# Opening of a two-sublayer decoder kernel on one core: four weight blocks in four equal strips in place of three blocks in five

## What is computed

```python
cond = silu(c)
mod = cond @ ada_w + ada_b                      # 2048 -> 9 * 2048
sh1, sc1, gt1, sh2, sc2, gt2, sh3, sc3, gt3 = split(mod, 9)
x = sandwich(x, swiglu(., ffn1_w_in, ffn1_w_out), sh1, sc1, gt1, 0.5)
x = sandwich(x, token_mixer(...),                 sh2, sc2, gt2, 1.0)
x = sandwich(x, swiglu(., ffn2_w_in, ffn2_w_out), sh3, sc3, gt3, 0.5)
# sandwich: x + res_w * gate * rms_norm(fn(rms_norm(x) * (1 + scale) + shift))
# swiglu(h): gate, up = split(h @ w_in, 2); (silu(gate) * up) @ w_out, hidden width 5504
```

## Time and profile before

| what | value |
|---|---|
| median of three timed runs | 1901.06 us (1900.74 to 1901.34) |
| the profiled execution's own time | 1902.87 us |
| its span, first to last instruction | 1901.1 us |
| busy: TensorE (PE), VectorE (DVE), ScalarE (ACT), GpSimd (POOL) | 98%, 77%, 45%, 4% |
| mean granted TensorE clock | 0.992 of full |
| read from memory over the span | 483.31 MB, 255 GB/s |

### The profile page before, as it was taken

The page is one execution under the profiler, slowest core; times in us unless marked ns, Lnnn a source line. Parts: engine busy times, 40 slices in busy tenths (PEclk is TensorE's granted clock), DMA queues, the critical chain, the costliest instruction groups (busy, mean ns, idle before and its releaser), DMA issues.

```text
span 1901.1 us, 21961 instructions
## 1 busy us (share of the span) xinstructions
PE 1857.7 (98%) x8775; PEld 1552.2 (82%) x8775; DVE 1469.8 (77%) x1569; ACT 857.0 (45%) x1095; POOL 81.7 (4%) x151
## 2 busy tenths in 40 slices
PE   6999999999999999999999999999999999999997
PEld 6888888888888889888778887888888888888895
DVE  5988889798888889975876587678877775676576
ACT  4244434434443444474666446544444434443443
POOL 0001000000000000010000010000000000000000
PEclk9989999999999999999999999999999999999999
DMA  9999999999999989745444454667776756556552
GB/s 369 371 355 362 355 340 337 367 332 339 347 344 343 371 326 343 271 147 187 155 133 133 161 175 158 231 235 242 244 250 237 243 185 198 193 198 212 176 200 78
DMA packets 208677, 486.84 MB, mean 256 GB/s; under 512 B 8560, under 2 KB 29760, under 8 KB 193472
## 3 DMA queue, kind: packets, MB, share of 16 engines
q1 hardware_dynamic: 191648, 365.72, 55.7%
q0 software_dynamic: 16224, 117.47, 16.8%
q10 hardware_dynamic: 704, 2.25, 0.3%
HBM read 483.31 MB, written 2.10 MB: 255 GB/s over the span
## 4 chain that ended last, share of the span: by engine, by line
PE 92%; DVE 4%; issue 1%; DMA 1%; ACT 1%; ACTq 0%; SPq 0%; DVEq 0%; POOL 0%
PE ps_u L1551 10%; PE ps_u L1553 10%; PE ps_u L1552 10%; PE ps_g L1551 10%; PE ps_g L1553 10%; PE ps_g L1552 10%; PE ps_t L1551 4%; PE ps_t L1553 4%; PE ps_t L1552 4%; PE ps_y L1551 4%; PE ps_y L1553 4%; PE ps_y L1552 4%; DVE arena L1267 1%; PE ps_g L1649 1%; DMA arena<-in_ada_w 1%
## 5 line engine op out<-in xcount | busy, mean ns | idle before, releaser
L595 ACT ACTIVATE w_hi<-w_raw 128x1024 fp32r<-128x1024 f32 (+2 forms) x604 | 628.4, 1042 | 875.1 <-PE ps_u L1553 306.5
L977 DVE TENSOR_TENSOR w_lo<-w_raw,w_hi 128x1024 fp32r<-128x1024 f32 (+2 forms) x604 | 719.5, 1199 | 341.7 <-ACT w_hi L595 339.6
L1551 PE MATMUL ps_u<-w_hi,xT_hi 128*128 128x512 f32 (+2 forms) x880 | 343.6, 390 | 2.6 <-DVE w_lo L1280 1.2
L1553 PE MATMUL ps_u<-w_hi,xT_lo 128*128 128x512 f32 (+2 forms) x880 | 339.1, 385 | 0.0
L1552 PE MATMUL ps_u<-w_lo,xT_hi 128*128 128x512 f32 (+2 forms) x880 | 338.8, 385 | 0.0
L1551 PE MATMUL ps_g<-w_hi,xT_hi 128*128 128x512 f32 (+1 forms) x816 | 318.8, 391 | 0.6 <-DVE w_lo L977 0.4
L1553 PE MATMUL ps_g<-w_hi,xT_lo 128*128 128x512 f32 (+1 forms) x816 | 315.0, 386 | 0.0
L1552 PE MATMUL ps_g<-w_lo,xT_hi 128*128 128x512 f32 (+1 forms) x816 | 314.6, 386 | 0.0
L1011 DVE SCALAR_TENSOR_TENSOR arena<-ada_raw,cond,arena 128x2048 f32<-128x2048 f32 x108 | 253.4, 2346 | 5.3 <-DMA ada_raw<-in_ada_w 5.3
L1551 PEld LDWEIGHTS ps_u<-w_hi,xT_hi 128*128 128x128 f32 x880 | 165.3, 188 | 35.9 <-issue 3.1
L1553 PEld LDWEIGHTS ps_u<-w_hi,xT_lo 128*128 128x128 f32 x880 | 165.3, 188 | 31.8
(11 more groups left out here) (320 smaller groups left out, 1885.2 us busy)
## 6 DMA issues: line engine op xcount, KB each, us to landing
w_raw<-in_ffn_w_in SPq DMA_DIRECT2D x157, 1024.0 KB, 6.4
ada_raw<-in_ada_w POOLq DMA_DIRECT2D x112, 1024.0 KB, 6.1
w_raw<-in_ffn_w_out SPq DMA_DIRECT2D x80, 1024.0 KB, 5.8
w_raw<-in_mix_w_in SPq DMA_DIRECT2D x32, 1024.0 KB, 5.0
ada_raw<-in_ada_w SPq DMA_DIRECT2D x32, 512.0 KB, 8.8
arena<-in_ada_w SPq DMA_DIRECT2D x32, 512.0 KB, 9.5
w_raw<-in_mix_w_out SPq DMA_DIRECT2D x16, 1024.0 KB, 5.0
w_raw<-in_ffn_w_in SPq DMA_DIRECT2D x16, 768.0 KB, 5.4
```

The costliest lines, as they stand in the source:

```text
L595: nc.scalar.activation(w_hi[:, u % 4, 0:n, 0:width], w_raw[:, s, 2 * hf:2 * hf + n, 0:width], ACT.Copy).then_inc(hi_done, 3 if g in EARLY_ ...
L977: nc.vector.tensor_tensor(w_lo[:, u % 4, 0:n, 0:width], w_raw[:, s, 2 * hf:2 * hf + n, 0:width], w_hi[:, u % 4, 0:n, 0:width].bitcast(F32) ...
L1551: nc.tensor.matmul(o, a_hi[:, k, rows], w_hi[:, b, c, 0:width], start=start, stop=False)
L1553: ins = nc.tensor.matmul(o, a_lo[:, k, rows], w_hi[:, b, c, 0:width], start=False, stop=stop)
```

## The change

- Four strips of four chunks instead of 4, 4, 4, 2, 2. Four blocks in each: up block 1 joins the other three, and group 3 is gone, so that the opening has 4 x 8 = 32 units where it had 24 and group 3 eight more.
- In PSUM there is no fifth pair, so up block 1 (`KEPT = 3`) uses `ps_y`, which the column sums also need. After its two units of a strip ScalarE copies the partial sum to SBUF (`save_partial`), and in the next strip TensorE puts it back with an identity matmul (`take_partial`), a float32 matmul of 512 columns for each of the two tiles: before the strip's first unit in strips 1 and 2, and in the last strip into `ps_u`, after the transposes of the first hidden block.
- `warm(32)` ahead of the column sums of strips 1 to 3; the other fillers inside the strips are gone.
- SP issues a strip's first weights ahead of the next strip's first tile. VectorE's order in a strip is written anew: units 0 and 1, columns, tile 0 of the next strip, rest of the input, unit 2, rest of the input, tile 1, units 3 and 4, tile 2, unit 5, tile 3, unit 6, tile 4, unit 7, tiles 5 to 7.
- The 96 later tiles of `ada_w` begin at unit 32 and go on every 11/5 units, the last at unit 241. The first ninth goes to another accumulator and is turned in hidden block 4 instead of 3. `start_acc` for the two gates comes later, between loads 36 and 37, and between loads 48 and 49.
- In group 4 the split of the transposed hidden block moves to the second unit, and the product for hidden block 1 to the fourth.

```diff
-ROWS_AT = (3, 5, 7, 9)
+ROWS_AT = (4, 5, 7, 9)
-STRIP_CHUNKS = ((0, 4), (4, 4), (8, 4), (12, 2), (14, 2))
+STRIP_CHUNKS = ((0, 4), (4, 4), (8, 4), (12, 4))
-OPENING = 3
+OPENING = 4
+KEPT = 3
-UNIT_FFN1 = [12 * a // 5 for a in range(6 * KD)]
+UNIT_FFN1 = [11 * a // 5 for a in range(6 * KD)]
...
+def block_of(s, i):
+    return (0, 3, 1, 2)[i] if s < STRIPS - 1 else i
...
-        ada_at = [8 * (G_FFN[0] + 3) + u for u in UNIT_FFN1]
+        ada_at = [8 * (G_FFN[0] + OPENING) + u for u in UNIT_FFN1]
...
             for s in range(STRIPS):
                 more = s + 1 < STRIPS
+                first_weights(s, 0)
                 if more:
                     first_tile(s + 1, 0)
...
             pool.wait_ge(modcol_done, STRIPS)
-            start_acc(2, 1)
-            start_acc(5, 0)
             for a in range(2, ADA_FFN2):
                 load_ada(a)
+                if a == 2 * KD + 4:
+                    pool.wait_ge(turned_done, 2)
+                    start_acc(2, 1)
+                if a == 3 * KD:
+                    start_acc(5, 0)
...
+            def save_partial(s):
+
+                act.wait_ge(pe_used, STRIP_UNITS * s + 4)
+                nc.scalar.activation(partial, ps_y[:, :, :], ACT.Copy).then_inc(partial_saved, 1)
...
+                lo_group(g0 + 4, 4, NB, {1: [ht_lo(0, 4, ps=ps_g)], 3: [h_mul(1, 0, NB, 8 * OPENING)],
+                                         4: [y_add(g0 + 4, y0, 0, True)], 6: [y_add(g0 + 4, y0 + 1, 1, True)]})
...
+                first_lo(start)
+                first_lo(start + 1)
+                first_columns(s)
+                if more:
+                    first_ada(s + 1, 0)
+                first_xt_lo(2 * s)
+                first_lo(start + 2)
+                first_xt_lo(2 * s + 1)
...
+            def take_partial(ps):
+                for t in range(TILES):
+                    nc.tensor.matmul(ps[:, t, :], ident[:, :], partial[:, t, :], start=True, stop=False)
...
-                    if i == units - 1 and s + 1 < STRIPS:
-                        warm((24, 24, 0, 0)[s], ps_y)
-                        first_sums(s + 1)
+                if s:
+                    pe.wait_ge(modcol_done, s + 1)
+                if s and not last:
+                    take_partial(ps_y)
...
+                    if last and b == KEPT and hf == 0:
+                        transpose_h(0, 4, 0, ps_g)
+                        take_partial(ps_u)
+                    if i == STRIP_UNITS - 1 and not last:
+                        pe.wait_ge(partial_saved, s + 1)
+                        warm(32, ps_y)
+                        first_sums(s + 1)
```

More of the change, by code:

```diff
@@ L1308, in _ @@
             for s in range(STRIPS):
[L1309 to L1325, removed]
-                    first_lo(start)
-                    first_xt_lo(first_xt)
-                    first_lo(start + 1)
-                    first_lo(start + 2)
-                    continue
+                start, more = STRIP_UNITS * s, s + 1 < STRIPS
                 first_lo(start)
@@ L1333, in _ @@
                 first_columns(s)
-                first_xt_lo(first_xt)
-                if tiles:
-                    first_ada(s + 1, 1)
-                    done = 2
-                for i in range(2, units):
-                    first_lo(start + i)
-                    if 2 * i - 2 < STRIP_CHUNKS[s][1]:
-                        first_xt_lo(first_xt + i - 1)
-                    late = i - units // 2 + 1
-                    upto = 2 + (tiles - 2) * late // (units - units // 2) if tiles and late > 0 else done
-                    for t in range(done, upto):
-                        first_ada(s + 1, t)
-                    done = upto
+                if more:
+                    first_ada(s + 1, 0)
+                first_xt_lo(2 * s)
+                first_lo(start + 2)
+                first_xt_lo(2 * s + 1)
+                if more:
+                    first_ada(s + 1, 1)
+                first_lo(start + 3)
+                first_lo(start + 4)
+                if not more:
+                    first_lo(start + 5)
+                    first_lo(start + 6)
+                    h_mul(0, 0, NB, start + 4)()
+                    first_lo(start + 7)
+                    continue
+                first_ada(s + 1, 2)
+                first_lo(start + 5)
+                first_ada(s + 1, 3)
+                first_lo(start + 6)
+                first_ada(s + 1, 4)
+                first_lo(start + 7)
+                for i in range(5, STRIP_TILES[s + 1]):
+                    first_ada(s + 1, i)
             ffn_dve(0)
@@ L1773, in first_sums @@
                         col = ps_y[:, 0, m * KD + k:m * KD + k + 1]
[L1774 removed]
+                        nc.tensor.matmul(col, even[:, s % 2, m, c * P:(c + 1) * P], ones[:, 0:1], start=True, stop=False)
                         ins = nc.tensor.matmul(col, odd[:, s % 2, m, c * P:(c + 1) * P], ones[:, 0:1], start=False, stop=True)
@@ L1795, in _ @@
             for s in range(STRIPS):
[L1796 to L1801 removed]
+                last = s == STRIPS - 1
+                if s:
+                    pe.wait_ge(modcol_done, s + 1)
+                if s and not last:
+                    take_partial(ps_y)
+                for i in range(STRIP_UNITS):
+                    v, (q, hf) = STRIP_UNITS * s + i, divmod(i, 2)
+                    b, pair = block_of(s, q), 2 * s + hf
+                    ps = (ps_g, ps_u, ps_t, ps_u if last else ps_y)[b]
+                    if last and b == KEPT and hf == 0:
[4 more added lines that the diff above has]
+                        warm(32, ps_y)
                         first_sums(s + 1)
[L1803 to L1806 removed]
                     pe.wait_ge(lo_done, v + 1)
```

129 lines of the change are left out of this document (46 added, 83 removed).

## The result

Over six timed runs each the changed kernel took 1909.19 us (median, 1903.83 to 1911.35), the kernel before 1901.2 (1899.06 to 1901.92). The ratio is 1.0042, with a 95% interval of 1.0032 to 1.0053. That is slower by 8 us, beyond the range's upper end of 1909 by 0.2 us and 1.2 us above the time that the prediction gave for its first rival (1908).

A forecast was written before the change was run, and what follows sets the result against it. TensorE's own work was taken to bound the kernel through the opening; 0.4 us of longer path plus 2.5 us of clock falls made 2.9 us, a median of 1904.0 us, range 1900 to 1909.

The forecast's parts named there:

- first rival: Unit 7 behind each column sums: the clock falls in every strip, 5.5 to 8 us, 1908 us; chance 0.20.
- Where the time is decided: Up to the end of the first layer: TensorE's own work bounds, and the opening can only shift the rest.
- pace: Behind the opening: a tile every 2.2 units instead of 2.4; VectorE's 58.1 of 66.2 us become 60.3, covered.
- transfers: Later tiles and weights: 24.0 MB in 66.2 us, 363 GB/s against 348 before, at cost 0.
- group 4: VectorE needs 23.3 us against TensorE's 21.8 but starts three units ahead; cost 0, bounds 0 and 1.5 us.
- the late starts of the accumulators: GpSimd's queue between later loads: a 7.1 us start makes load 49 1.7 us late; cost 0, bound 1.
- The sum of the parts: TensorE from 49.85 us to the end of unit 31: 123.2 us against 122.8, so 0.4 us later.
- The account of before: The same stretch in the kernel before: 122.8 us of units, fillers, column sums, waits, transposes and slow clock.
- VectorE and the tiles keep up: Each opening strip: VectorE takes 27.6 us against TensorE's 30.9, 3.3 us ahead; late tiles cost 0, bounds 0 and 1.7.
- The clock: Behind the opening's column sums: one or two falls to half clock in three strips, 2.5 us.
- Strip length: Opening, from one strip's sums to the next: 34.5 us; over 37 us would show the forecast wrong.
- The tiles end at unit 241 instead of 252, which gives TensorE nothing: End of the later `ada_w` tiles: ending earlier gains no time, because TensorE does not wait there.

The follow-up runs named there:

- the split kernel: The changed kernel with the column sums of strips 1 to 3 in two halves around the first half of unit 7; 1902.7 us, ratio 1.0010.
- 16 fillers: The changed kernel with column sums in halves, the next strip's first tile summed ahead of the columns, and 16 filler matmuls instead of 32; 1904.99 us.
- the kernel before split: The kernel before with 28 and 35 filler matmuls instead of 24 and 24, column sums of its second and third strip in halves; 1900.5 us.
- 22 fillers: The changed kernel with column sums in halves, the next strip's first tile summed ahead of the columns, and 22 filler matmuls instead of 32; 1902.34 us.
- 18 fillers: The changed kernel with column sums in two halves and 18 filler matmuls instead of 32; 1905.43 us, ratio 1.0027.
- the one with 18 fillers: The changed kernel with 18 filler matmuls instead of 32 and nothing else, sums in one piece; 1900.11 us, ratio 0.9999.

## Why the prediction was wrong, point by point

- **Where the time is decided.** Right. TensorE has no wait from 43 to 720 us, the rest of the kernel is as long as before within 0.4 us, and pace, transfers (362 GB/s against 363 forecast), group 4 and the late starts of the accumulators cost nothing. The limit of about 358 GB/s that the Trainium skill gives (DMA: Bandwidth & Descriptors, Specifications) was passed, at 362 GB/s over 520 us, without a wait of TensorE.
- **The sum of the parts.** Right for the kernel after. A restoring took 1.7 us (79.98 to about 81.7), the filler 7.1 (7.36 forecast), the sums 3.5 (3.6). The kernel without falls takes 123.1 us for the forecast 123.2, its own wait of 0.9 us left out. The account of before does not close: the named terms (84.3, 13.9, 10.8, 5.3, 0.8 and 6.7) are 121.8 of 122.8 us. So what the change spends (8.2 + 5.2) less what it gives back (5.3 + 6.7) is 1.4 us and not the 0.4 of the other way of counting, a gap too small to matter here.
- **VectorE and the tiles keep up.** Right for this kernel, ahead by 3.6, 3.2 and 3.2 us (3.3 forecast). The agreement is partly luck: ahead of the second and the third sums it stands behind a fall, which the 3.3 us left out and which holds TensorE up. In the split kernel, with the same filler and no falls, VectorE was only 1.4 us ahead there.
- **The clock: the step that failed.** "I take one or two falls in three strips: 2.5 us." All three profiled strips fell, for 3.4, 7.2 and 7.0 us, and this cost 8.3 us; in the run that only splits the sums no strip falls, and 6.5 us come back net of its new wait of 0.9. The mechanism was named, and so was the rival that had it right (a fall in every strip, 5.5 to 8 us, 1908), with a chance of 0.20. The rows spoke for it more than I allowed. The only stretch in them without a fall had sums half as long; the two full-length ones had both ended slow, and one of them after a wait of only 0.77 us. I let the missing wait decide. The runs show that 3.5 us of unbroken column sums are enough without a wait (the changed kernel, and the kernel before with its waits filled), and that behind a wait of 2.3 us or more the falls are longer (10.1 us in the kernel before; in the kernel without filler the whole of the sums and of unit 7).
- **Strip length.** 34.5 us from sums to sums was forecast, and over 37 us named as a sign of being wrong. The two strips took 35.8 and 37.5 us; without falls (the split kernel) they take 34.3. The sign showed, by way of the clock and not of the transfers.
- **"The tiles end at unit 241 instead of 252, which gives TensorE nothing."** Right against the kernel before, but incomplete. The start had moved from unit 24 to 32; at the old pace the tiles end at unit 260, and the part behind `w_out` was 3.7 us longer in the profiled run. The new pace is a needed companion of the later start.
- **The range.** Rival 1's own upper price, 0.4 + 8 us on 1901.06, is 1909.5, which the range of 1900 to 1909 left out. The cost of the clock also differs from one execution to the next: one and the same kernel took 1903.83 to 1911.35 us.

Open: what decides when a fall begins and how long it lasts. With equal work ahead, the falls of the changed kernel's profiled run begin 4.1, 2.5 and 2.4 us after the first of the sums. Open too is whether a filler of large products would keep the clock better than one of 128-column matmuls; no run tried it.

## What to carry to other kernels

Where the clock is concerned, price a stretch of one-column matmuls as a wait although the profile shows TensorE busy, add it to the waits that touch it, and break it up with real matmuls before adding filler. A filler on the path of the bounding engine costs its whole length: size it by how far ahead the next engine is, read from the trace, and size it anew after every edit, since the clock that it keeps changes who is late. Where the work of two engines has nearly the same period, gains on one of them don't add up.

## What the hardware showed that I had not expected

- Behind sums of 3.5 us that directly follow 7.1 us of filler, the clock fell in all three strips of the profiled run, and so in the runs with the other order of SP's queue and without restoring; with the same work cut into 1.7 + 1.5 (products) + 1.7 us it did not fall in any.
- Waits of 0.56, 0.61, 0.84, 1.27 and 1.7 us ahead of such halves came with a fall (16 fillers, the kernel before split, 22 fillers, 16 and 18 fillers); one of 0.34 us (16 fillers, third strip) did not.
- Two kernels with the sums in one piece spread over 7.5 and 9.1 us from run to run (the changed one and the one with 18 fillers), two without any fall over 1.5 and 2.0 us. It is no rule: without restoring, with a fall in each strip, the spread was 2.4 us.
